# One step of a streaming encoder on one core: the first norm's sum is merged on VectorE and its root becomes one power on GpSimd

## The reference, cut to what matters

```python
def rmsnorm(x, g):
    xf = x.astype(jnp.float32)
    xf = xf * lax.rsqrt(jnp.mean(xf * xf, axis=-1, keepdims=True) + NORM_EPS)
    return (xf * g.astype(jnp.float32)).astype(x.dtype)
...
n1 = rmsnorm(h, lw['g_mix'])
z = n1 @ lw['w_in']          # q, k, v, u, g_a, g_b
```

## Time and profile before

| | |
|---|---|
| median of 3 timed runs | 1670.67 us (1670.61 to 1670.88) |
| the profiled execution's span, first to last instruction | 1668.5 us |
| what lies around the span in a timed run, median less span | 2.2 us |
| TensorE busy / mean granted clock | 1656.9 us (99%) / 0.998 |
| VectorE / ScalarE / GpSimd busy | 853.3 / 671.9 / 81.2 us |

### The profile page before, as it was taken

One profiled execution on the slowest core, in us unless ns is written; L12 is line 12 of the kernel. 1 busy time (PEld: TensorE's weight loads), 2 busy tenths in 40 slices (PEclk: granted clock), 3 DMA queues, 4 the chain that ended last, 5 costly groups with the idle time before them and its releaser, 6 DMA issues.

```text
span 1668.5 us, 28875 instructions
## 1 busy us (share of the span) xinstructions
PE 1656.9 (99%) x11292; PEld 1646.6 (99%) x11292; DVE 853.3 (51%) x1185; ACT 671.9 (40%) x978; POOL 81.2 (5%) x73
## 2 busy tenths in 40 slices
PE   9999999999999999999999999999999999999997
PEld 8999999999999999999999999999999999999997
DVE  7569544444445557444344443344433444555765
ACT  6355534333333444443333333333323344444442
POOL 2434000000000004000000000000000000000000
PEclk9999999999999999999999999999999999999999
DMA  9433544444445444444444444444444444444431
GB/s 350 165 127 127 212 145 147 146 148 149 151 151 191 151 151 152 146 146 145 145 150 148 150 151 151 151 151 151 151 148 145 147 146 148 147 151 151 152 126 63
DMA packets 41305, 255.44 MB, mean 153 GB/s; under 512 B 5808, under 2 KB 8752, under 8 KB 11696
## 3 DMA queue, kind: packets, MB, share of 16 engines
q1 hardware_dynamic: 37184, 246.86, 41.6%
q10 hardware_dynamic: 4080, 8.03, 1.3%
HBM read 250.30 MB, written 4.58 MB: 153 GB/s over the span
## 4 chain that ended last, share of the span: by engine, by line
PE 99%; DVE 0%; DMA 0%; issue 0%; DVEq 0%; ACTq 0%; ACT 0%
PE acc L500 32%; PE acc L501 32%; PE acc L502 32%; DVE h L1421 0%; PE sm_ps L551 0%; PE o_ps L566 0%; DMA p_first<-in_p_in 0%; PE t_ps L534 0%; PE acc L582 0%; PE sm_ps L582 0%; PE o_ps L680 0%; PE sm_ps L514 0%; PE o_ps L582 0%; PE t_ps L582 0%; PE t_ps L680 0%; PE sm_ps L691 0%
## 5 line engine op out<-in xcount | busy, mean ns | idle before, releaser
L711 ACT ACTIVATE w_hi<-raw 128x1024 fp32r<-128x1024 f32 x460 | 486.5, 1059 | 885.8 <-PE acc L502 885.2
L500 PE MATMUL acc<-xa_hi,w_hi 128*128 128x320 f32 x2112 | 654.2, 310 | 0.0
L502 PE MATMUL acc<-xa_hi,w_lo 128*128 128x320 f32 x2112 | 652.6, 309 | 0.0
L501 PE MATMUL acc<-xa_lo,w_hi 128*128 128x320 f32 x2112 | 652.6, 309 | 0.0
L993 DVE TENSOR_TENSOR w_lo<-raw,w_hi 128x1024 fp32r<-128x1024 f32 x460 | 547.3, 1229 | 5.0 <-ACT w_hi L711 4.8
L500 PEld LDWEIGHTS acc<-xa_hi,w_hi 128*128 128x128 f32 x2112 | 396.5, 188 | 2.3 <-issue 1.5
L501 PEld LDWEIGHTS acc<-xa_lo,w_hi 128*128 128x128 f32 x2112 | 396.5, 188 | 0.2
L502 PEld LDWEIGHTS acc<-xa_hi,w_lo 128*128 128x128 f32 x2112 | 396.5, 188 | 0.0
L501 PE MATMUL acc<-xb_lo,w_hi 128*128 128x320 f32 x1280 | 395.5, 309 | 0.0
L500 PE MATMUL acc<-xb_hi,w_hi 128*128 128x320 f32 x1280 | 395.5, 309 | 0.0
L502 PE MATMUL acc<-xb_hi,w_lo 128*128 128x320 f32 x1280 | 395.5, 309 | 0.0
(11 more groups left out here) (223 smaller groups left out, 912.4 us busy)
## 6 DMA issues: line engine op xcount, KB each, us to landing
raw<-in_weights SPq DMA_DIRECT2D x228, 1024.0 KB, 4.7
raw<-in_weights SPq DMA_DIRECT2D x5, 512.0 KB, 9.3
h<-in_x SPq DMA_DIRECT2D x8, 320.0 KB, 8.4
h<-in_x ACTq DMA_DIRECT2D x1, 2560.0 KB, 10.1
out_y<-h ACTq DMA_DIRECT2D x7, 320.0 KB, 2.6
e_spill<-e_first SPq DMA_DIRECT2D x1, 1280.0 KB, 12.1
e<-e_spill ACTq DMA_DIRECT2D x1, 1280.0 KB, 6.1
raw<-in_weights SPq DMA_DIRECT2D x2, 256.0 KB, 4.3
```

The lines of the kernel that those rows point to most:

```text
L500: nc.tensor.matmul(out, w_hi[:, at:at + P], x_hi[:, m * T:(m + 1) * T], start=k == 0, stop=False)
L501: nc.tensor.matmul(out, w_hi[:, at:at + P], x_lo[:, m * T:(m + 1) * T], start=False, stop=False)
L502: mm = nc.tensor.matmul(out, w_lo[:, at:at + P], x_hi[:, m * T:(m + 1) * T], start=False, stop=k == depth - 1)
L711: nc.scalar.activation(w_hi[:, dst:dst + HALF], raw[:, src:src + HALF], ACT.Copy).then_inc(hi_done, 1)
```

## The change

VectorE adds `odd_sum` to `sumsq` itself (semaphore `xall`), between the first and the second half of unit 4's `w_lo`, and TensorE sums one source in place of two. ScalarE's square root, VectorE's reciprocal and the three Newton instructions of the first norm are gone. In their place GpSimd raises the mean plus epsilon to the power of minus one half in one instruction over 128 x 320, with the exponent read from a tile of constants (`minus_half`). VectorE waits for that result (`root_first`) before it writes out unit 1. The mean is formed behind the second half of unit 4's `w_lo`. The counts of the later norms move down, since the first one no longer raises `n_std` and `n_r`.

```diff
@@ gpsimd
             nc.gpsimd.memset(odd_sum, 0.0).then_inc(xodd, 1)
+            nc.gpsimd.memset(minus_half[:, :], -0.5).then_inc(half_set, 1)
...
             pool.wait_ge(xodd, KD // 2 + 1)
+            pool.wait_ge(half_set, 1)
+            pool.wait_ge(n_var, 1)
+            nc.gpsimd.tensor_tensor(r[:, :], sumsq[:, :], minus_half[:, 0:1].broadcast_to([P, T]), ALU.pow).then_inc(root_first, 1)
@@ tensor
                     pe.wait_ge(ev_act, KA // 2)
-                    pe.wait_ge(xadd, KD // 2)
-                    pe.wait_ge(xodd, KD // 2 + 1)
-                    partition_sum(0, sumsq[:, :], odd_sum)
+                    pe.wait_ge(xall, 1)
+                    partition_sum(0, sumsq[:, :])
@@ scalar
-            root(0, sumsq, r)
             for u in range(U_KV + 2, U_STEP):
                 ahead(u, u)
@@ vector
-            ahead(U_KV + 1, U_KV + 1)
+            ahead(U_KV + 1, U_KV + 1, [0])
+            dve.wait_ge(xadd, KD // 2)
+            dve.wait_ge(xodd, KD // 2 + 1)
+            nc.vector.tensor_tensor(sumsq[:, :], sumsq[:, :], odd_sum, ALU.add).then_inc(xall, 1)
             for line in (kx, vx):
                 nc.vector.memset(line.rearrange("p (n k) -> p n k", n=NPAIR)[:, :, 2 * CHUNK:3 * CHUNK], 0.0)
-            inverse_root(0, sumsq, r)
-            newton(0, sumsq, r)
+            ahead(U_KV + 1, U_KV + 1, [1])
+            dve.wait_ge(n_mm, 1)
+            nc.vector.tensor_scalar(sumsq[:, :], sums[0][:, 0:T], 1.0 / D, EPS, ALU.mult, ALU.add).then_inc(n_var, 1)
             ahead(U_KV + 2, U_KV + 2, [0])
 
             for n, line in enumerate((kx, vx)):
                 for p in range(NPAIR):
                     u = n * NPAIR + p
                     dve.wait_ge(used, 2 * (U_KV + u) + 2)
+                    dve.wait_ge(root_first, 1)
```

More of the change, by code:

```diff
@@ L220, in encoder_step @@
         e_sq = sb("e_sq", T)
-        last_var, last_r = sb("last_var", NL), sb("last_r", NL)
+        last_var, last_r, minus_half = sb("last_var", NL), sb("last_r", NL), sb("minus_half", 4)
         part_hi, part_lo, ones_r = sb("part_hi", T, F32R), sb("part_lo", T, F32R), sb("ones_r", P, F32R)
-        sb("unused", 4 * KA * T - KD * T - 3 * KP * T - T - 2 * T - P - NL * 2)
+        sb("unused", 4 * KA * T - KD * T - 3 * KP * T - T - 2 * T - P - NL * 2 - 4)
         with ExitStack() as early:
@@ L297, in encoder_step @@
         xadd, xodd = sem("xadd"), sem("xodd")
+        xall, half_set, root_first = sem("xall"), sem("half_set"), sem("root_first")
         n_mm = sem("n_mm")
@@ L687, in _ @@
                 nc.tensor.matmul(o_ps[:, :], w_hi[:, 0:P], xa_hi[:, 0:4 * P], start=True, stop=True)
-            pe.wait_ge(n_r, 4 * 5)
+            pe.wait_ge(n_r, 4 * 4)
             for i, at in enumerate(LAST_BLOCKS):
@@ L1015, in inverse_root @@
                 mean.then_inc(n_var, 1)
-                dve.wait_ge(n_std, n + 1)
+                dve.wait_ge(n_std, n)
                 nc.vector.reciprocal(out[:, 0:cols], out[:, 0:cols]).then_inc(n_r, 1)
@@ L1020, in newton @@
                 v, f = var[:, 0:cols], out[:, 0:cols]
-                dve.wait_ge(n_r, 4 * n + 1)
+                dve.wait_ge(n_r, 4 * n - 3)
                 nc.vector.tensor_tensor(v, v, f, ALU.mult).then_inc(n_r, 1)
-                dve.wait_ge(n_r, 4 * n + 2)
+                dve.wait_ge(n_r, 4 * n - 2)
                 nc.vector.scalar_tensor_tensor(out=v, in0=v, scalar=-0.5, in1=f,
                                                op0=ALU.mult, op1=ALU.mult).then_inc(n_r, 1)
-                dve.wait_ge(n_r, 4 * n + 3)
+                dve.wait_ge(n_r, 4 * n - 1)
                 nc.vector.scalar_tensor_tensor(out=f, in0=v, scalar=1.5, in1=f,
                                                op0=ALU.add, op1=ALU.mult).then_inc(n_r, 1)
-                dve.wait_ge(n_r, 4 * n + 4)
+                dve.wait_ge(n_r, 4 * n)
             def part_low(n, of):
```

## The result

The changed kernel takes 1719.24 us (1718.77 to 1719.35, 4 runs) against 1670.64 us (1670.35 to 1670.88, 4 runs) for the kernel before, a ratio of 1.0291 with a 95% interval of 1.0278 to 1.0304. It is 48.6 us slower, where I forecast 1670.5 us and a range up to 1678.

The account below looks back on a forecast made before the run. TensorE, busy in 99% of the span, was taken as the bound. Single sum -0.53, new wait +0.21 and power's delay +0.1 gave -0.2 us, from 1670.67 to about 1670.5 us, range 1670.0 to 1678.0.

Parts of the forecast that it names:

- D: Length of GpSimd's power in the first norm, not shown by any row; taken as 3.9 us.
- S: TensorE's delay ahead of unit 5 from the power, its length less 3.8 us; 0.1 us in the sum.
- a long power: Rival: power of 7.5 us or more makes TensorE wait before unit 5; at 8.5 us net +4.4 us; chance 0.31.
- Branching: GpSimd's power: data-dependent branching at about 12 cycles an element, estimated 3.2 us on top of a loop, so near 4.
- The gain on TensorE: At the first norm's sum, one source in place of two takes 0.53 us out of TensorE's stream.
- The loss of 0.21 us: Before the sum, TensorE newly waits for VectorE's extra add; 0.21 us, between 0.1 and 0.35.
- The collision: GpSimd's power and VectorE's `w_lo` for unit 5 don't run side by side; together 1.2 us plus the power's length.
- In either order: Whichever of the power and unit 5's `w_lo` goes first, the two take 1.2 us plus the power's length.
- The cover of 3.8 us: Before unit 5, the power may last 3.8 us without delaying TensorE; anything longer delays it one for one.
- The clock: Added to the long-power rival: a wait of 4.7 us may lower TensorE's clock, about 1.7 us lost; no separate chance.
- Late code: Rival: the power's code must be fetched first, making it 7.4 us, wait 3.6, net +3.3 us; chance 0.06.
- ScalarE: With its root removed, ScalarE makes unit 5's high parts some 3 us earlier; costed at nothing.

Follow-up runs that it names:

- 48 columns: The changed kernel with GpSimd's power over 48 columns only, VectorE setting the rest of the factor to 1; 1675.92 us (one run).
- 96: The changed kernel with GpSimd's power over 96 columns only, VectorE setting the rest of the factor to 1; 1683.19 us (one run).
- the run with the powers of other sizes: The changed kernel with eight more powers and one multiply on GpSimd in front of the change's own power; 1863.29 us (one run).
- 20 and the `w_lo` in front: The changed kernel with the power over 20 columns, the rest of the factor set to 1, `w_lo` not moved behind the wait; 1669.85 us (one run).

## Why the prediction was wrong

**The step that failed is the length of the power.** The prediction bounded D by 0.88 us below and 8.5 us above, took 3.9 (S = 0.1 in the sum), and called a longer one possible "with no bound from rows". It is 51.3 us undisturbed, 6 times the upper bound. The scaling from VectorE's reciprocal had no basis: there a reciprocal costs 4.4 multiplies, and on GpSimd a power costs 57 (25.82 against 0.45 us at 160 columns). The range then reached 1678 on a bound that was itself a guess. The case that came true is the rival "a long power", by its own formula: the delay is D less 3.8 us, 51.3 - 3.8 = 47.5, as measured (how far that cover was luck stands below). I gave it 0.31 and cut it off near 10 us.

**Branching.** From the Trainium skill ("GPSIMD Engine Reference", "Elementwise — side-by-side cycle accounting") I had estimated about 4 us, taking its 12 cycles an element as 12 cycles a column. The page counts the same way: in that section an add of 2048 elements takes 4497 ns, which at the 1.2 GHz of its "Specifications" is 2.6 cycles a column. The runs show 0.159 us a column, 191 cycles at that clock and 16 times the page's 12. The page gives a core 16 partitions ("Specifications"), and 191 / 16 is 12, but a price for each partition doesn't explain the runs: one partition alone costs as much as 128. A base of exactly 1 costs as much as the data. So whether branching is the cause remains open.

**The gain on TensorE** was right at 0.53 us, though behind a wait that ends with the power it buys nothing. The loss of 0.21 us against it did not come: VectorE's add started at 34.65 and the sum's first matmul at 35.34 in the changed kernel, against 35.0 and 35.47 taken from before. From the start of unit 4's first `w_lo` to unit 3's last matmul it is 2.06 us in the kernel before, 2.26 in the changed one and 2.39 with the merged sum alone, so the phase of the two engines moved by as much as that term.

**The collision** was half right. A `w_lo` that is already running holds GpSimd's start back by 0.83 us; a power that runs held VectorE back by 0.32 us near its start and by nothing behind it. "In either order" was wrong. The cover of 3.8 us for the power's own time came out all the same, and that is luck, since four of its terms were off and cancel. The power started at 37.05 and not 37.47, and the `w_lo` held it for 0.83 and not 1.21 us; against that, unit 5 was due at 42.93 and not 43.26, and VectorE started 0.53 us behind the power's end, which no term had. With the 1.24 us from the power's end to TensorE's first matmul, 42.93 - 37.05 - 0.83 - 1.24 = 3.8 us. The same sum gives 4.1 us with 48 columns and 4.4 with 96. The prediction's other value, 5.0 us if `w_lo` keeps to 1.2 us (which it did), was out as well: for the power's recorded length the cover was 52.16 - 47.5 = 4.6 us. The Trainium skill ("SBUF — State Buffer", "SBUF: two separate sides") has the pair locked for a whole instruction, and the sixteen subtracts inside one power contradict that for the power; the measurement decides.

**The clock** went as the rival had it: it fell in the pause and cost 1.9 us (1.7 forecast). The prediction counted that cost from a wait of 4.7 us on; the run with 48 columns paid 1.6 us behind a wait of 3.8.

**Late code** is out: the first power of a launch costs nothing extra once the `w_lo` is out of its way (3.54 us, the line's 3.53).

**ScalarE** did make unit 5's high parts early (the last one started at 35.53 us, where the pair began at 37.65), and it bought nothing, as costed.

## What to carry to other kernels

Don't scale the cost of an instruction that no trace shows from another engine; if the cover is 3.8 us and the length is unknown, the range must say so, or the instruction has to be measured by itself first. GpSimd's power costs 0.16 us a column however few partitions it has, so 20 columns of it fit the cover here and 48 don't. A factor that is equal on all partitions is the worst layout for it: with the 320 frames spread over the partitions it would be 3 columns, by the line an estimate of 0.35 + 3 x 0.159 = 0.8 us, which no run here tried and which leaves out the cost of spreading them. A stall of the engine that sets the end cost its length here and 1.6 to 2.3 us of clock on top, in the run with a wait of 3.8 us as in the longer ones. And work saved in front of such a stall is no gain by itself: it makes the wait longer, unless what is waited for starts earlier by it.

## What the runs showed of the hardware that I had not expected

A GpSimd power of 128 x 320 takes 51.3 us, while a multiply takes 0.72, and its time doesn't depend on partitions (25.81 us for 1 or 16 of them and 25.82 for 128, at 160 columns). VectorE's two-operand subtracts ran at their full 1.216 us inside such a power (16 of them in 51.7 us), though beside one of GpSimd's adds such a subtract took 1.78 us. The power's end and the start of the VectorE instruction that waits for it are 0.53 us apart in the changed kernel (89.21 to 89.74) and in the run with the powers of other sizes, but 0.10 us behind the equally long power of the run with the power alone, 0.09 with 48 columns, with 96 and with 20 and the `w_lo` in front, and 0.03 behind the one of 3.54 us (40.88 to 40.91). What that gap is stays open.
